# A seventh buffer for gate and up weights, in two parts, and three sets of gathered rows in a routed expert phase

## The chip, the cores and the metric

The kernel runs on one core of one Trainium2 chip. Its time is device microseconds (us) of one execution. Before the change it is 1276.21 us, the median of 3 runs (1276.14 to 1276.45). One execution was profiled: it took 1278.38 us, and its trace spans 1276.8 us. All positions below ("at 1066.34") are us from the start of that span.

## The reference, cut to what matters

One layer of an encoder for 1024 prompt frames and 32 sample frames: two kinds of attention side by side, and then a mixture of experts. Only the mixture and the routing ahead of it are touched by the order of the work. Everything is float32.

```python
def hier_moe(h, w_rg, b_rg, w_re, b_re, w_gate, w_up, w_down):
    g_sel = argmax(softmax(h @ w_rg + b_rg))            # 1 of 4 groups
    top_i = top_k(e_logits[g_sel], 2)                   # 2 of its 8 experts
    a = einsum('sd,edf->sef', h, w_gate)                # D_MODEL 1024, D_EXPERT 256, 32 experts
    b = einsum('sd,edf->sef', h, w_up)
    act = silu(a) * b * gates[:, :, None]
    return einsum('sef,efd->sd', act, w_down)
```

An expert's weights are w_gate and w_up (1 MiB each) and w_down (1 MiB): 96 MiB for the 32 experts.

## The kernel before, in words

The kernel is a row of phases. `phase_fr` (L1953) multiplies the attention's outputs with w_out, norms, and routes each frame to two experts; it writes the normed rows to `h2_dram` and the lists of (row, weight) per expert to `list_dram`. `phase_g` computes the experts. Between phases all engines meet.

`expert_blocks()` cuts the experts' lists into 23 blocks of 128 rows. Experts are named by a position p: 0 to 3 are known when the program is written, 17 and 31 (EARLY) are known early in routing, all others come from a table that routing sorts. The blocks, with the positions whose rows they hold: 0: 17+31; 1: 0; 2: 13+27; 3: 1; 4: 5+22; 5: 6+22; 6: 7+22; 7: 19+8; 8: 20+8; 9: 21+8; 10: 2; 11: 14+28; 12: 3; 13: 15+29; 14: 9+26; 15: 10+26; 16: 11+26; 17: 4; 18: 23+12; 19: 24+12; 20: 25+12; 21: 18; 22: 16+30.

For a block b GpSimd gathers 128 rows (`rows_in`, an indirect DMA, L2682) into one of ROWSETS = 4 sets of rows, PE turns them (`rows_turned`, g_X, L2689), PE multiplies them with gate and up weights (`first_products`, g_GU, L2697), ScalarE and VectorE form the hidden rows, PE turns these (g_H, L2704) and multiplies them with the down weights (`second_products`, g_Y, L2714), VectorE weights the result (L2940) and GpSimd adds it to `y` (`results_out`, L2676). PE's order is written out: in turn b it does first_products(b), second_products(b-1), rows_turned(b+2), hidden_turned(b); in the last turns second_products(21) comes ahead of first_products(22). GpSimd does rows_in(s) and then results_out(s - LAG), LAG being ROWSETS + 2.

Weights lie in six buffers, each with a part for gate and up (`w_gu`, 16 KB a partition) and a part for down (`w_down`, 8 KB a partition). An expert gets one buffer for both (`place`), the one whose present holder's last block comes first; `instead[p]` is that last block. SyncE (SP) issues all weight loads from one queue in program order: `gate_up_in(p)` waits until gu_mm has counted block instead[p] and issues two DMAs of 1 MiB (L2552, L2553), `down_in(p)` waits for dn_mm likewise and issues one (L2558). A down load is put off until its wait is two blocks older than that of the next gate and up load:

```python
            for p in order[len(known):]:
                while left and instead[left[0]] + 2 <= instead[p]:
                    down_in(left.pop(0))
                gate_up_in(p)
                left.append(p)
```

The four known experts and the gate and up weights of 17 and 31 are issued in phase_fr, the down weights of 17 and 31 (d17, d31) at the start of phase_g when the first gathered rows are in. After them SP's order is, with g for a gate and up pair (2 MiB) and d for a down load (1 MiB):

g13 g27 g5 d13 d27 g22 g6 d5 g7 d22 d6 g19 d7 g8 d19 g20 g21 d8 g14 d20 d21 g28 d14 g15 g29 d28 g9 d15 d29 g26 g10 d9 g11 d26 d10 g4 g23 d11 g12 d4 d23 g24 d12 g25 g18 d24 g16 d25 d18 g30 d16 d30.

"Position n" of a load in this order means the MiB issued from g13 on, itself included: g13 is at 2, g27 at 4, d5 at 13, d22 at 16, g8 at 22, d19 at 23, d8 at 28, d26 at 52, d12 at 65, d24 at 70, d25 at 73, d30 at 78.

Of the kernel before, what the change touches and what calls it, by code (L numbers as in the profile page):

```python
# [31 lines left out]
P = 128  # L32
D = 1024
KD = D // P
# [33 lines left out]
ROWW = _at  # L68
# [1884 lines left out]
def phase_fr(nc, io, g):  # L1953

    with ExitStack() as stack:
# [141 lines left out]
        @block.gpsimd  # L2097
        def _(pool):
            step = Steps(pool, pool_step)
            step(nc.gpsimd.iota(rown, pattern=[[1, LROWS]], base=0, channel_multiplier=LROWS))  # L2100
            step(nc.gpsimd.iota(i32[:], pattern=[[1, NE]], base=0, channel_multiplier=0))
            for k in range(2):
                step(nc.gpsimd.iota(pair[:, :, k, 0], pattern=[[P, NT]], base=0, channel_multiplier=1))
            for xg in g.xg:
                nc.gpsimd.memset(xg[:], 0.0)
            pool.wait_ge(oT_mm, 1)
            nc.gpsimd.memset(g.sample_region[:], 0.0)
            pool.wait_ge(z_out, 16)
# [484 lines left out]
def phase_g(nc, io, g):  # L2593

    with ExitStack() as stack:
        m = Memory(nc, stack)
        FT = DE // P
        ROWSETS = 4
        HALVES = (slice(0, D // 2), slice(D // 2, D))
        blocks = expert_blocks()  # L2600
        NB = len(blocks)
        wgu, wd = g.w_gu, g.w_down
        SLOTS = len(wgu)
# [8 lines left out]
        place, nth, instead = {}, {}, {}  # L2612
        holding = {}
        known = list(range(FIXED)) + list(EARLY)
        order = known + [p for p in order if p not in known]
        for q, p in enumerate(order):
            s = q if q < SLOTS else min(holding, key=lambda x: last_block[holding[x]])
            instead[p] = last_block[holding[s]] if q >= SLOTS else None
            nth[p] = sum(1 for x in place if place[x] == s)
            place[p], holding[s] = s, p  # L2620
        li = g.li + [m.sb(f"g_li{b}", [P, 2], U32) for b in range(3, NB)]
        l_li = m.sb("g_l_li", [P, 2], U32)
        xg = g.xg + [g.early[:, 0:D], g.sample_region]
        spare = 2 * KD * DE + 2 * D
        xT = g.first_region[:, spare:spare + 2 * KD * P].rearrange("p (b k t) -> p b k t", b=2, k=KD)
        sig = m.sb("g_sig", [P, DE])
# [12 lines left out]
        xT_mm, xT_done, gu_mm, sig_done, hid_done, hT_mm, hT_done, dn_mm, y_done, st_y, dve_step, started, l_side = m.sems(  # L2639
            "g_xT_mm g_xT_done g_gu_mm g_sig_done g_hid_done g_hT_mm g_hT_done g_dn_mm g_y_done g_st_y g_dve_step "  # L2640
            "g_started l_side")
# [50 lines left out]
        def gate_up(b, slots):  # L2692

            n = P // len(slots)
            for k in range(KD):
                for h, s in enumerate(slots):
                    end = nc.tensor.matmul(GU[h * n:h * n + n, :], lhsT=xT[:, b, k, h * n:h * n + n], rhs=wgu[s][:, :, k, :],  # L2697
                                           start=k == 0, stop=k == KD - 1, tile_position=(0, h * n))
            return end

# [18 lines left out]
        def lists(b):  # L2719
            return 16 * len(blocks[b])  # L2720

        def slots_of(b):

            unit = min(n for _, _, n, _ in blocks[b])
            return [place[p] for p, _, n, _ in blocks[b] for _ in range(n // unit)]

        @block.sync
        def _(sp):
            experts = {r: r * EPG for r in range(FIXED)}

            def expert(r):
                if r not in experts:
                    experts[r] = sp.value_load(g.order[0:1, r:r + 1], min_val=0, max_val=NE - 1)
                return experts[r]

            def gate_up_in(p):
                sp.wait_ge(gu_mm, instead[p] + 1)
                load_gate_up(nc, io, g, sp, expert(p), place[p], wgu_in[place[p]])

            def down_in(p):  # L2740
                sp.wait_ge(dn_mm, instead[p] + 1)
                load_down(nc, io, g, sp, expert(p), place[p], wd_in[place[p]])

            for b in (1, 2):
                load_list(g, sp, blocks[b], {p: expert(p) for p, *_ in blocks[b]}, li[b], li_in[b])
            sp.wait_ge(xg_in[0], 16)
            for p in EARLY:
                load_down(nc, io, g, sp, expert(p), place[p], wd_in[place[p]])
# [62 lines left out]
        def _(pe):  # L2811
            def first_products(b):
                for p, _, _, _ in blocks[b]:
                    pe.wait_ge(wgu_in[place[p]], 32 * nth[p] + 32)
                pe.wait_ge(xT_done, b + 1)
                if b:
                    pe.wait_ge(hid_done, b)
                gate_up(b % 2, slots_of(b)).then_inc(gu_mm, 1)

            def rows_turned(b):  # L2820
                pe.wait_ge(xg_in[b % ROWSETS], 16 * (b // ROWSETS) + 16)
# [3 lines left out]

            def second_products(b):
                for p, _, _, _ in blocks[b]:
                    pe.wait_ge(wd_in[place[p]], 16 * nth[p] + 16)
                pe.wait_ge(hT_done, b + 1)
                if b >= 2:  # L2830
                    pe.wait_ge(y_done, b - 1)
                if b == NB - 1:
                    down(b % 2, slots_of(b), lambda half: half.then_inc(dn_mm, 1)).then_inc(dn_mm, 1)
                else:
                    down(b % 2, slots_of(b)).then_inc(dn_mm, 1)

            def hidden_turned(b):
                pe.wait_ge(hid_done, b + 1)
# [168 lines left out]
def program(nc, io):  # L3007
    USED.clear()
    g = Shared()
    with ExitStack() as stack:  # L3010
# [14 lines left out]
        g.tri = m.sb("tri", [P, P])  # L3025
        g.ones = m.sb("ones", [P, P])
        g.eps = m.sb("eps", [P, 1])
        g.rows = m.sb("rows", [P, ROWW])
# [3 lines left out]
        g.ckv_new = m.sb("ckv_new", [P, KR])  # L3032
        g.vecT = m.sb("vecT", [P, 80])
        g.silu_c = m.sb("silu_c", [P, KD, 32])
# [62 lines left out]
        g.wgu_in = m.sems("wgu_in0 wgu_in1 wgu_in2 wgu_in3 wgu_in4 wgu_in5")  # L3097
        g.wd_in = m.sems("wd_in0 wd_in1 wd_in2 wd_in3 wd_in4 wd_in5")
        g.w_gu, g.w_down = [], []

# [11 lines left out]
        g.xg = [m.sb(f"g_xg{r}", [P, D]) for r in range(2)]  # L3112
        g.li = [m.sb(f"g_li{b}", [P, 2], U32) for b in range(3)]
        g.li_in = m.sems("g_li_in0 g_li_in1 g_li_in2")
        g.late = m.sb("late", [P, 12 * D])
        for part in (g.late[:, 0:6 * D], g.late[:, 6 * D:]):
            g.w_gu.append(part[:, 0:2 * KD * DE].rearrange("p (w k n) -> p w k n", w=2, k=KD))
            g.w_down.append(part[:, 2 * KD * DE:].rearrange("p (k n) -> p k n", n=D))
        phase_fr(nc, io, g)
        phase_g(nc, io, g)  # L3120
        mixed.close()
# [43 lines left out]
```

## Time and profile before

| what | value |
|---|---|
| median of 3 runs | 1276.21 us |
| the profiled execution | 1278.38 us |
| its span | 1276.8 us |
| PE busy over the span | 1165.3 us, 91% |
| VectorE, ScalarE, GpSimd busy | 714.7, 350.7, 214.6 us |
| expert phase, first gather to end | 967.8 to 1276.8 |

In the page, "PE" is the matrix engine, "SPq" SyncE's queue of instructions. An idle time ahead of an instruction is shown in square brackets with what ended it; "issue" means that the trace shows no releaser. A wait for a weight load often shows so, since the landing of such a load has no record of its own for each buffer. "DMA" in a table by stretches is the mean busy share of the core's 16 DMA engines.

### The profile page before, as it was taken

How to read it: one execution, taken by the hardware profiler on the slowest of the kernel's cores; microseconds unless marked ns; L12 is line 12 of the kernel's file. 1: busy time of each engine (PE TensorE's matmuls, PEld its weight loads, DVE VectorE, ACT ScalarE, POOL GpSimd, SP SyncE). 2: the span in 40 equal slices, each digit the busy share in tenths (PEclk: the TensorE clock that was granted, in tenths of full speed). 3: DMA queues.
4: the chain of work that ended last, by engine and by line, in shares of the span. 5: the costliest groups of instructions: out<-in, count | busy, mean ns of one | idle time of the engine just before them, and what ended most of it. 6: DMA issues, size and time to landing. Idle time of an engine off the chain costs nothing. (4 is left out here: it accounts for less than half of the span.)

```text
span 1276.8 us, 18764 instructions
## 1 busy us (share of the span) xinstructions
PE 1165.3 (91%) x7144; PEld 655.0 (51%) x7145; DVE 714.7 (56%) x1386; ACT 350.7 (27%) x770; POOL 214.6 (17%) x250
## 2 busy tenths in 40 slices
PE   4899999999968997799999999899976998999996
PEld 1456455564544556566677767555553332343332
DVE  1647476573756885467777686544472353544444
ACT  1113132141223444266555544223331000000000
POOL 0000000000400002254443333010122121222111
PEclk9899999999988998789999999899986999999998
DMA  8802223032257879421111005362565999999993
GB/s 362 328 17 88 71 61 114 17 88 59 67 158 237 300 276 274 124 60 30 30 30 31 1 1 168 97 246 84 192 250 179 398 382 369 363 388 391 351 327 79
DMA packets 103275, 226.17 MB, mean 177 GB/s; under 512 B 21034, under 2 KB 61212, under 8 KB 87826
## 3 DMA queue, kind: packets, MB, share of 16 engines
q1 hardware_dynamic: 92562, 207.61, 45.3%
q0 software_dynamic: 7344, 17.33, 5.5%
q8 instruction: 58, 0.95, 0.3%
q10 hardware_dynamic: 3280, 0.02, 0.1%
q14 instruction: 31, 0.25, 0.1%
HBM read 192.37 MB, written 39.38 MB: 182 GB/s over the span
## 5 line engine op out<-in xcount | busy, mean ns | idle before, releaser
L2142 PE MATMUL f_C<-first_region,oT 128*128 128x512 f32 x256 | 114.7, 601 | 0.0
L2922 DVE TENSOR_TENSOR g_sig<-g_GU,g_sig 128x256 f32<-128x256 f32 x23 | 9.8, 425 | 156.3 <-ACT g_sig L2873 156.3
L2697 PE MATMUL g_GU<-w_gu,first_region 128*32 128x512 f32 (+2 forms) x448 | 86.1, 604 | 6.0 <-issue 4.8
L2697 PE MATMUL g_GU<-late,first_region 128*32 128x512 f32 (+2 forms) x384 | 87.6, 606 | 4.3 <-issue 4.3
L1922 DVE TENSOR_TENSOR_SCAN region<-region,early 128x128 f32<-128x128 f32 (+7 forms) x64 | 88.5, 1403 | 5.0 <-POOL region L1726 4.9
L2142 PEld LDWEIGHTS f_C<-first_region,oT 128*128 128x128 f32 x256 | 47.8, 192 | 54.0 <-issue 53.8
L2676 POOL DMA_INDIRECT y<-oT,g_li x22 | 34.9, 1586 | 216.3 <-DVE oT L2940 208.7
L1791 PE MATMUL e_Z<-first_region,region 104*128 104x512 f32 (+3 forms) x192 | 70.5, 505 | 0.3 <-ACT region L1884 0.3
L1734 POOL TENSOR_SCALAR region<-region,e_sm 128x128 f32<-128x128 f32 (+7 forms) x64 | 47.0, 745 | 130.3 <-DVE e_sm L1935 130.3
L457 POOL MEMSET first_region<- 8x8448 f32 x1 | 7.1, 7132 | 316.0 <-PE U L495 316.0
L1928 DVE TENSOR_REDUCE e_sm<-e_Z 128x1 f32<-128x128 f32 (+7 forms) x64 | 46.5, 747 | 23.1 <-PE e_Z L1791 22.1
L2873 ACT ACTIVATE g_sig<-g_GU 128x256 f32<-128x256 f32 x23 | 8.8, 383 | 181.4 <-PE g_GU L2697 181.4
L1884 ACT ACTIVATE region<-e_Z,e_sm 128x128 f32<-128x128 f32 (+7 forms) x64 | 47.2, 749 | 11.3 <-DVE e_sm L1928 11.2
L2697 PEld LDWEIGHTS g_GU<-w_gu,first_region 128*32 128x32 f32 (+2 forms) x448 | 25.2, 119 | 48.0 <-issue 46.0
L1791 PEld LDWEIGHTS e_Z<-first_region,region 104*128 104x128 f32 x192 | 33.8, 198 | 29.8 <-issue 26.5
L495 PE MATMUL U<-first_region,values 128*128 128x512 f32 x96 | 44.9, 612 | 2.5 <-DVE values L893 2.5
L1862 ACT ACTIVATE region<-e_Z 128x128 f32<-128x128 f32 (+7 forms) x64 | 38.1, 649 | 33.0 <-PE e_Z L1770 33.0
L2714 PE MATMUL g_Y<-late,early 128*32 128x512 f32 (+2 forms) x192 | 45.3, 615 | 0.7 <-ACT early L2876 0.7
L2697 PEld LDWEIGHTS g_GU<-late,first_region 128*32 128x32 f32 (+2 forms) x384 | 25.8, 125 | 38.3 <-issue 37.9
L1770 PE MATMUL e_Z<-region 64*128 64x512 f32 (+3 forms) x192 | 41.1, 533 | 4.5 <-ACT region L1884 2.4
L1726 POOL TENSOR_SCALAR region<-region 128x128 f32<-128x128 f32 (+7 forms) x64 | 42.0, 672 | 14.2 <-ACT region L1862 13.2
L2113 POOL DMA_INDIRECT list_dram<-f_pair,f_dest x18 | 19.4, 1080 | 145.2 <-DVE f_dest L2505 142.5
(550 smaller groups left out, 2399.8 us busy)
## 6 DMA issues: line engine op xcount, KB each, us to landing
region<-w_ada SPq DMA_DIRECT2D x16, 1024.0 KB, 6.3
late<-w_gate SPq DMA_DIRECT2D x14, 1024.0 KB
late<-w_up SPq DMA_DIRECT2D x14, 1024.0 KB
late<-w_down SPq DMA_DIRECT2D x14, 1024.0 KB
w_gu<-w_gate SPq DMA_DIRECT2D x12, 1024.0 KB
w_gu<-w_up SPq DMA_DIRECT2D x12, 1024.0 KB
w_down<-w_down SPq DMA_DIRECT2D x12, 1024.0 KB, 21.5
region<-w_in SPq DMA_DIRECT2D x3, 2048.0 KB, 17.2
```

The lines of the kernel that those rows point to most:

```text
L495: end = nc.tensor.matmul(dst[:, :], lhsT=rows[:, k, :], rhs=weights(k), start=k == 0, stop=k == HALF - 1)
L1726: nc.gpsimd.tensor_scalar(part, part, -0.5, 0.5, ALU.mult, ALU.add).then_inc(left_done, 1)
L1734: nc.gpsimd.tensor_scalar(part, part, sm[:, n % 2, 4 + hh:5 + hh], 1.0, ALU.mult, ALU.mult).then_inc(scaled, 1)
L1770: end = nc.tensor.matmul(Z[:, hh, at + c:at + c1], lhsT=q_s[r, b, p, :], rhs=keys[r, p, c:c1], start=True, stop=True)
L1791: end = nc.tensor.matmul(Z[:, hh, at + c:at + c1], lhsT=g.q_hidden[:, b, h, :], rhs=g.kT_hidden[:, h, c:c1], start=True, stop=True)
L1862: nc.scalar.activation(stick[:, n % 2, hh, 0:W], Z[:, hh, at:at + W], ACT.Tanh, scale=0.5 * SB_SCALE).then_inc(tanh_done, 1)
L1884: nc.scalar.activation(w[:, hh, to:to + W], Z[:, hh, at:at + W], ACT.Exp, bias=sm[:, n % 2, hh:hh + 1], accum_out=sm[:, n % 2, 2 + hh:3 + ...
L1922: nc.vector.tensor_tensor_scan(back, back, least, 1.0, ALU.mult, ALU.max).then_inc(scan_done, 1)
L1928: nc.vector.tensor_reduce(sm[:, n % 2, hh:hh + 1], Z[:, hh, at:at + (t + 1) * P], AX.X, ALU.max, negate=True).then_inc(max_done, 1)
L2142: end = nc.tensor.matmul(C[n % 2][:, c * 512:(c + 1) * 512], lhsT=g.oT[:, i, k, :], rhs=wo[:, k, c * 512:(c + 1) * 512], start=k == 0, sto ...
L2697: end = nc.tensor.matmul(GU[h * n:h * n + n, :], lhsT=xT[:, b, k, h * n:h * n + n], rhs=wgu[s][:, :, k, :], start=k == 0, stop=k == KD - 1 ...
L2714: end = nc.tensor.matmul(Y[b][h * n:h * n + n, c * 512:(c + 1) * 512], lhsT=hT[:, b, k, h * n:h * n + n], rhs=wd[s][:, k, c * 512:(c + 1) ...
```

## The change

- There are seven places for gate and up weights and still six for down weights. The two kinds are planned apart (`plan(APART + 1)`, `plan(APART)`), so an expert's gate and up weights and its down weights can lie in different buffers.
- The seventh place is in two parts of 8 KB a partition each, `g.passing` and `g.apart`; four of the eight k slices of gate and up lie in each. Five experts land in it: 13, 7, 14, 11, 16. Their loads are four DMAs of 512 KB, with 4 KB a partition, instead of two of 1 MiB.
- `g.passing` also holds what earlier phases use (tri, ones, rows, ckv_new, vecT, silu_c), each of which was a tensor of its own. `g.apart` takes the room of two row sets.
- ROWSETS is 3: the sets are early, sample_region and a new tensor of phase_g. GpSimd clears the new one at the start of phase_g, ahead of its first gather; the clearing of two sets in phase_fr is gone. LAG becomes 5.

```diff
-            for xg in g.xg:
-                nc.gpsimd.memset(xg[:], 0.0)
...
-        ROWSETS = 4
+        ROWSETS = 3
...
-        for q, p in enumerate(order):
-            s = q if q < SLOTS else min(holding, key=lambda x: last_block[holding[x]])
-            instead[p] = last_block[holding[s]] if q >= SLOTS else None
+        def plan(buffers):
+            place, nth, instead, holding = {}, {}, {}, {}
+            for q, p in enumerate(order):
+                s = q if q < buffers else min(holding, key=lambda x: last_block[holding[x]])
+                instead[p] = last_block[holding[s]] if q >= buffers else None
+                nth[p] = sum(1 for x in place if place[x] == s)
+                place[p], holding[s] = s, p
+            return place, nth, instead
+
+        place_gu, nth_gu, instead_gu = plan(APART + 1)
+        place_d, nth_d, instead_d = plan(APART)
+
+        def weights_at(s, k):
+            return wgu[s][:, :, k, :] if s < APART else g.two_parts[k // (KD // 2)][:, :, k % (KD // 2), :]
+
+        def two_halves(name, e):
+            return io[name][e].rearrange("(p c k) n -> p c k n", p=P, c=2)
+
+        def gate_up_count(p):
+            return (32 if place_gu[p] < APART else 64) * (nth_gu[p] + 1)
...
-        xg = g.xg + [g.early[:, 0:D], g.sample_region]
+        xg = [g.early[:, 0:D], g.sample_region, m.sb("g_xg2", [P, D])]
...
             def gate_up_in(p):
-                sp.wait_ge(gu_mm, instead[p] + 1)
-                load_gate_up(nc, io, g, sp, expert(p), place[p], wgu_in[place[p]])
+                if instead_gu[p] is not None:
+                    sp.wait_ge(gu_mm, instead_gu[p] + 1)
+                if place_gu[p] < APART:
+                    load_gate_up(nc, io, g, sp, expert(p), place_gu[p], wgu_in[place_gu[p]])
+                    return
+                for w, name in enumerate(("w_gate", "w_up")):
+                    for c, part in enumerate(g.two_parts):
+                        sp.dma_start(part[:, w], two_halves(name, expert(p))[:, c]).then_inc(wgu_in[APART], 16)
...
-                while left and instead[left[0]] + 2 <= instead[p]:
+                while left and instead_gu[p] is not None and instead_d[left[0]] + 2 <= instead_gu[p]:
                     down_in(left.pop(0))
...
         def _(pool):
+            nc.gpsimd.memset(xg[2][:], 0.0).then_inc(cleared, 1)
+
             def rows_in(b):
+                if b == 2:
+                    pool.wait_ge(cleared, 1)
```

SP's order after d17 and d31 follows from the two plans:

g13 g27 g5 g22 d13 d27 g6 g7 d5 g19 d22 d6 g8 d7 g20 d19 g21 g14 d8 g28 d20 d21 g15 d14 g29 g9 d28 g26 d15 d29 g10 g11 d9 g4 d26 d10 g23 g12 d11 g24 d4 d23 g25 d12 g18 g16 d24 g30 d25 d18 d16 d30.

In it g13 has no wait on a block; g27 and g5 wait for block 0, g22 for block 1, d13 and d27 for block 0's second products; g21 and g14 wait for block 6.

## Rows read from the trace of the kernel before

**Rows 1.** The page: busy time of PE over the span.
```profile
PE 1165.3 (91%) x7144; PEld 655.0 (51%) x7145; DVE 714.7 (56%) x1386; ACT 350.7 (27%) x770; POOL 214.6 (17%) x250
```

**Rows 2.** Busy time by stretches: start:end length, engines, PEclk, DMA share, GB/s.
```profile
986.00:1230.00 244.00, 230.73 (x1540) 91.86 (x1544) 106.80 (x155) 15.31 (x40) 49.01 (x38) 0.99 1.01 375
974.00:990.00 16.00, 14.28 (x57) 6.56 (x57) 4.43 (x5) 0.77 (x2) 4.95 (x5) 0.80 0.68 232
780.00:785.00 5.00, 5.00 (x64) 4.26 (x59) 3.33 (x6) 1.89 (x6) 2.22 (x2) 1.00 1.05 398
```

**Rows 3.** Timeline of PE in the expert phase, instructions with idle time ahead.
```profile
1002.59 0.65 PE L2697 MATMUL g_GU<-late,first_region 128*64 128x512 f32 x2 [2.96 <-issue]
...
1066.34 1.07 PE L2697 MATMUL g_GU<-w_gu,first_region 128*32 128x512 f32 x3 [4.84 <-issue]
...
1152.56 0.63 PE L2697 MATMUL g_GU<-oT,first_region 128*32 128x512 f32 x3 [2.40 <-issue]
...
1171.88 0.63 PE L2714 MATMUL g_Y<-oT,early 128*32 128x512 f32 x3 [0.34 <-issue]
...
1201.68 0.63 PE L2697 MATMUL g_GU<-late,first_region 128*32 128x512 f32 x3 [1.29 <-issue]
...
1214.62 0.63 PE L2697 MATMUL g_GU<-w_gu,first_region 128*32 128x512 f32 x3 [1.12 <-DMA w_gu<-w_up]
```

**Rows 4.** DMA queues, 986 to 1230: packets, MB, share of 16 engines.
```profile
q1 hardware_dynamic: 10606, 77.30, 78.0%
q0 software_dynamic: 5328, 14.04, 22.0%
```

**Rows 5.** Single down loads on SP's queue: time of issue, then us to landing.
```profile
L2558 SPq DMA_DIRECT2D w_down<-w_down x1: 333/333/333, 1013.3 to 1013.3; - x1
DMA to landing us min/median/max: 19.3/19.3/19.3
...
L2558 SPq DMA_DIRECT2D w_down<-w_down x1: 333/333/333, 1048.5 to 1048.5; - x1
DMA to landing us min/median/max: 21.5/21.5/21.5
...
L2558 SPq DMA_DIRECT2D w_down<-w_down x1: 2245/2245/2245, 1137.1 to 1137.1; - x1
DMA to landing us min/median/max: 34.7/34.7/34.7
...
L2558 SPq DMA_DIRECT2D oT<-w_down x1: 3671/3671/3671, 1182.8 to 1182.8; - x1
DMA to landing us min/median/max: 34.3/34.3/34.3
...
L2558 SPq DMA_DIRECT2D w_down<-w_down x1: 2053/2053/2053, 1211.1 to 1211.1; - x1
DMA to landing us min/median/max: 31.0/31.0/31.0
```

**Rows 6.** GpSimd: the clearing of two row sets; the first gather of phase_g.
```profile
L2105 POOL MEMSET g_xg<- x2: 957/958/959, 792.0 to 792.9; 128x1024 f32 x2
...
967.78 1.04 POOL L2682 DMA_INDIRECT g_xg<-h_dram,g_li  x1 [8.21 <-DMA g_li<-list_dram]
```

**Rows 7.** Chain of waits: start, us, what.
```profile
1044.98 3.43 PE g_Y L2714 x32
...
1066.34 8.42 PE g_GU L2697 x64
...
1086.53 3.43 PE g_Y L2714 x32
...
1091.29 7.00 PE g_GU L2697 x64
...
1233.46 3.43 PE g_Y L2714 x32
```

**Rows 8.** Clock: stretch with the longest wait; columns as in rows 2.
```profile
1060.00:1070.00 10.00, 5.16 (x38) 2.40 (x38) 2.88 (x3) 0.38 (x1) 2.62 (x2) 0.83 1.03 390
```

**Rows 9.** DMA issues 850 to 1277: KB each, us to landing.
```profile
h_dram<-late SPq DMA_DIRECT2D x6, 512.0 KB, 2.7
```

More of the change, by code:

```diff
@@ L2602, in phase_g @@
         wgu, wd = g.w_gu, g.w_down
-        SLOTS = len(wgu)
+        APART = len(wgu)
         order = []
@@ L2611, in phase_g @@
                 last_block[p] = b
-        place, nth, instead = {}, {}, {}
-        holding = {}
         known = list(range(FIXED)) + list(EARLY)
         order = known + [p for p in order if p not in known]
-        for q, p in enumerate(order):
-            s = q if q < SLOTS else min(holding, key=lambda x: last_block[holding[x]])
-            instead[p] = last_block[holding[s]] if q >= SLOTS else None
-            nth[p] = sum(1 for x in place if place[x] == s)
-            place[p], holding[s] = s, p
+        def plan(buffers):
[14 more added lines that the diff above has]
+            return (32 if place_gu[p] < APART else 64) * (nth_gu[p] + 1)
         li = g.li + [m.sb(f"g_li{b}", [P, 2], U32) for b in range(3, NB)]
         l_li = m.sb("g_l_li", [P, 2], U32)
-        xg = g.xg + [g.early[:, 0:D], g.sample_region]
+        xg = [g.early[:, 0:D], g.sample_region, m.sb("g_xg2", [P, D])]
         spare = 2 * KD * DE + 2 * D
@@ L2638, in phase_g @@
         Y = [m.ps(f"g_Y{b}", [P, D]) for b in range(2)]
-        xT_mm, xT_done, gu_mm, sig_done, hid_done, hT_mm, hT_done, dn_mm, y_done, st_y, dve_step, started, l_side = m.sems(
+        xT_mm, xT_done, gu_mm, sig_done, hid_done, hT_mm, hT_done, dn_mm, y_done, st_y, dve_step, started, l_side, cleared = m.sems(
             "g_xT_mm g_xT_done g_gu_mm g_sig_done g_hid_done g_hT_mm g_hT_done g_dn_mm g_y_done g_st_y g_dve_step "
-            "g_started l_side")
+            "g_started l_side g_cleared")
         wgu_in, wd_in = g.wgu_in, g.wd_in
@@ L2696, in gate_up @@
                 for h, s in enumerate(slots):
-                    end = nc.tensor.matmul(GU[h * n:h * n + n, :], lhsT=xT[:, b, k, h * n:h * n + n], rhs=wgu[s][:, :, k, :],
+                    end = nc.tensor.matmul(GU[h * n:h * n + n, :], lhsT=xT[:, b, k, h * n:h * n + n], rhs=weights_at(s, k),
                                            start=k == 0, stop=k == KD - 1, tile_position=(0, h * n))
@@ L2720, in lists, with slots_of @@
             return 16 * len(blocks[b])
-        def slots_of(b):
+        def slots_of(b, place):
             unit = min(n for _, _, n, _ in blocks[b])
@@ L2736, in gate_up_in @@
             def gate_up_in(p):
-                sp.wait_ge(gu_mm, instead[p] + 1)
-                load_gate_up(nc, io, g, sp, expert(p), place[p], wgu_in[place[p]])
+                if instead_gu[p] is not None:
[6 more added lines that the diff above has]
+                        sp.dma_start(part[:, w], two_halves(name, expert(p))[:, c]).then_inc(wgu_in[APART], 16)
             def down_in(p):
-                sp.wait_ge(dn_mm, instead[p] + 1)
-                load_down(nc, io, g, sp, expert(p), place[p], wd_in[place[p]])
+                sp.wait_ge(dn_mm, instead_d[p] + 1)
+                load_down(nc, io, g, sp, expert(p), place_d[p], wd_in[place_d[p]])
             for b in (1, 2):
@@ L2747, in _ @@
             for p in EARLY:
-                load_down(nc, io, g, sp, expert(p), place[p], wd_in[place[p]])
+                load_down(nc, io, g, sp, expert(p), place_d[p], wd_in[place_d[p]])
             left = []
             for p in order[len(known):]:
-                while left and instead[left[0]] + 2 <= instead[p]:
+                while left and instead_gu[p] is not None and instead_d[left[0]] + 2 <= instead_gu[p]:
                     down_in(left.pop(0))
@@ L2813, in first_products @@
                 for p, _, _, _ in blocks[b]:
-                    pe.wait_ge(wgu_in[place[p]], 32 * nth[p] + 32)
+                    pe.wait_ge(wgu_in[place_gu[p]], gate_up_count(p))
                 pe.wait_ge(xT_done, b + 1)
@@ L2817, in first_products @@
                     pe.wait_ge(hid_done, b)
-                gate_up(b % 2, slots_of(b)).then_inc(gu_mm, 1)
+                gate_up(b % 2, slots_of(b, place_gu)).then_inc(gu_mm, 1)
             def rows_turned(b):
@@ L2827, in second_products @@
                 for p, _, _, _ in blocks[b]:
-                    pe.wait_ge(wd_in[place[p]], 16 * nth[p] + 16)
+                    pe.wait_ge(wd_in[place_d[p]], 16 * nth_d[p] + 16)
                 pe.wait_ge(hT_done, b + 1)
@@ L2832, in second_products @@
                 if b == NB - 1:
-                    down(b % 2, slots_of(b), lambda half: half.then_inc(dn_mm, 1)).then_inc(dn_mm, 1)
+                    down(b % 2, slots_of(b, place_d), lambda half: half.then_inc(dn_mm, 1)).then_inc(dn_mm, 1)
                 else:
-                    down(b % 2, slots_of(b)).then_inc(dn_mm, 1)
+                    down(b % 2, slots_of(b, place_d)).then_inc(dn_mm, 1)
             def hidden_turned(b):
@@ L3024, in program @@
         g.ident = m.sb("ident", [P, P])
-        g.tri = m.sb("tri", [P, P])
-        g.ones = m.sb("ones", [P, P])
+        g.passing = m.sb("passing", [P, 2 * D])
+        g.tri = g.passing[:, D:D + P]
+        g.ones = g.passing[:, D + P:D + 2 * P]
         g.eps = m.sb("eps", [P, 1])
-        g.rows = m.sb("rows", [P, ROWW])
+        g.rows = g.passing[:, 0:ROWW]
         g.modT = m.sb("modT", [P, 48, 2])
@@ L3031, in program @@
         g.scale_m = m.sb("scale_m", [P, KD, 2])
-        g.ckv_new = m.sb("ckv_new", [P, KR])
-        g.vecT = m.sb("vecT", [P, 80])
-        g.silu_c = m.sb("silu_c", [P, KD, 32])
+        g.ckv_new = g.passing[:, D + 2 * P:D + 2 * P + KR]
+        g.silu_c = g.passing[:, D + 4 * P:D + 6 * P].rearrange("p (k b) -> p k b", b=32)
+        g.vecT = g.passing[:, D + 6 * P:D + 6 * P + 80]
         g.w_in_loaded = m.sems("w_lat_loaded w_v_loaded w_q_loaded w_k_loaded")
@@ L3096, in program @@
         g.longest = m.sb("longest", [1, 1], I32)
-        g.wgu_in = m.sems("wgu_in0 wgu_in1 wgu_in2 wgu_in3 wgu_in4 wgu_in5")
+        g.wgu_in = m.sems("wgu_in0 wgu_in1 wgu_in2 wgu_in3 wgu_in4 wgu_in5 wgu_in6")
         g.wd_in = m.sems("wd_in0 wd_in1 wd_in2 wd_in3 wd_in4 wd_in5")
@@ L3111, in program @@
         g.y = turned[:, 6 * KD * P:8 * KD * P].rearrange("p (b n) -> p b n", b=2)
-        g.xg = [m.sb(f"g_xg{r}", [P, D]) for r in range(2)]
+        g.apart = m.sb("apart", [P, 2 * D])
         g.li = [m.sb(f"g_li{b}", [P, 2], U32) for b in range(3)]
@@ L3118, in program @@
             g.w_down.append(part[:, 2 * KD * DE:].rearrange("p (k n) -> p k n", n=D))
+        g.two_parts = [part[:].rearrange("p (w k n) -> p w k n", w=2, k=KD // 2) for part in (g.passing, g.apart)]
         phase_fr(nc, io, g)
```

## The prediction

> **What bounds the kernel now.** I read the page first, then the stretches, then PE's timeline, then the loads. PE is busy 91% of the span [rows 1], and in the expert phase, 986 to 1230, it is busy 230.7 of 244 us while the 16 DMA engines are at 1.01, that is full [rows 2]. Both are near their limit, so the question is which one waits for the other. PE's timeline answers: it has six idle times there, five ahead of first products and one ahead of second products, of 2.96, 4.84, 2.40, 0.34, 1.29 and 1.12 us, 12.95 us in all [rows 3]. Behind the longest the clock has fallen (0.83 in that stretch, between its levels of 2.4 and 1.2 GHz) [rows 8], and the first products take 8.42 us instead of 7.00, another 1.42 [rows 7]. So 14.37 us of this phase are PE waiting for weights.
>
> That they are waits for loads in their order is seen by counting positions. The six waits end at position 4 (g27), 22 (g8), 46 (g26), 52 (d26), 60 (g12) and 64 (g24). From 1002.59 to 1066.34 that is 63.75 us for 18 MiB, 3.54 us each; from 1066.34 to 1214.62 148.3 us for 42, 3.53 each [rows 3]. Single down loads lie on the same line: d5 (13) lands at 1013.3 + 19.3 = 1032.6, d19 (23) at 1070.0, d26 (52) at 1171.8, d12 (65) at 1217.1, d25 (73) at 1242.1 [rows 5]. SP's loads are one stream, delivered in order of issue at a steady pace from 986 to about 1230. A buffer more can't make the stream faster. It can start it earlier, and it changes who stands ahead of whom in it.
>
> **Part 1: the earlier start.** g13 no longer waits for block 0; it follows d17 and d31. From 974 to 990 the DMA engines are at 0.68, so 16 x 0.32 = 5.1 us of them are idle [rows 2]. The loads' own pace is 77.30 MB in 0.78 x 244 = 190 us, 406 GB/s [rows 2, 4], so g13 (2.10 MB) needs 5.2 us and just fits. Against it stands part 2. I take 4.0 us of lead for the whole stream; between 0 (nothing of the gap used) and 5.1.
>
> **Part 2: the clearing.** It now stands ahead of GpSimd's first gather, at the point where all engines wait for it. It takes 0.96 us, and the gather starts at 967.78 with PE idle behind it [rows 6]. I take the whole 0.96 us, for the first rows, for d17, d31 and g13; it could be 0 if it fits under the wait for the list, and is hardly over 1.1. That part of the lead is taken off in the 4.0. The clearing removed from phase_fr lay beside PE's work: 0.
>
> **Part 3: the order.** Compare the two orders: every down load from d13 to d18 now has two MiB more ahead of it. d22 goes from position 16 to 18, d8 from 28 to 30, d26 from 52 to 54, d24 from 70 to 72. Gate and up loads stand up to 2 MiB earlier (g8 22 to 21, g26 46 to 44, g12 60 to 59, g24 64 to 62). Two MiB are 5.2 us at 406 GB/s, the lead is 4.0: the down loads land 1.2 us later than before. So the gate and up loads are out of the way, and the question becomes how much room the down loads had.
>
> **Part 4: half pieces.** Five experts load in pieces of 512 KB with 4 KB a partition. w_out, loaded with 2 KB a partition, moved at 398 GB/s [rows 2], against 406. For 10 MiB that is 26.3 against 25.8 us: between 0 and 0.5, I take 0.3 by d24, 0.15 by d8, behind a filled queue. The far end is a piece that overlaps nothing: 2.7 us from issue to landing [rows 9] against 1.3 us of moving, 1.4 us for each of 20 pieces, 28 us; with several MiB outstanding all the time I give that nothing. SP's ten additional issues lie beside a full queue: 0.
>
> **Part 5: three row sets.** Gather b is issued behind result b-6 instead of b-7, and is needed in turn b-2, three turns (35 us) later: not late. One gather fewer stands beside the stream at a given moment. Queue 0 takes 22% of 244 us for 38 gathers and result transfers [rows 2, 4], 1.4 us each. So between 0 and -1.4 for a down load in the middle; I take -0.7, and 0 for d24, by when all gathers are done either way.
>
> **The sum, turn by turn.** Offsets are to the profiled execution.
> - Block 2: before, ready at 1002.59 - 2.96 = 999.63, waited for g27. Now ready at 1000.6; g27 lands 4 us earlier, 998.6. No wait. Offset -2.0.
> - Second products of block 4 started at 1044.98 [rows 7], now ready at 1043.0. They need d22: before, at 1032.6 + 3 x 3.74 = 1043.8 (3.74 us each between d5 and d19). Now 1.2 + 0.1 - 0.7 = 0.6 later, 1044.4. Wait 1.4, offset -0.6.
> - First products of block 7: the 4.84 and the 1.42 are gone (g8, at 21, about 1058.6). Second products of block 7 are ready at 1086.53 - 4.84 - 1.42 - 0.6 = 1079.7. They need d8. Six MiB behind g8, at (1171.8 - 1070.0) / 29 = 3.51 each, it is due at 1087.4; PE did not wait at 1086.53 [rows 7], so it landed just before. I take 1086.5, and now 0.7 later, 1087.2. Wait 7.5 us. A wait longer than 4.84 brings the clock down again: +1.4. Offset +2.1.
> - Block 14: the 2.40 is gone (g26 at 44), offset -0.3. Its second products, ready at 1171.54 - 0.3 = 1171.2, need d26: 1171.8 + 0.7 = 1172.5. Offset +0.6.
> - Blocks 18 and 19: 1.29 and 1.12 gone. Offset -1.8.
> - Second products of block 19 started at 1233.46 [rows 7], now ready at 1231.7. They need d24. Before, between d12 (65) and d25 (73), 3.13 us each: 1232.7. Now 1.2 + 0.3 later, 1234.2. Wait 2.5. Offset +0.7.
> - d25 (1242.1 before) and later ones have their room, and the tail is unchanged.
>
> The span becomes 1276.8 + 0.7 = 1277.5 and the profiled time 1279.1. The medians lie 2.2 us below that execution, so 1276.21 + 0.7 = 1276.9 us. The 14.4 us of waits for gate and up weights turn into about 12 us of waits for down weights, the clearing and the clock.
>
> Bounds: d24 before at the earliest 1230.1 (1217.1 + 5 x 2.6, nothing beside the stream) and at the latest 1233.46; its delay between 0 and 5.7. d26's delay is at least -1.4, which leaves the start of block 14's second products at 1170.4, offset -1.5, and -3.9 after the two waits that go. So -3.9 to +5.8.
>
> **The rivals.**
> - *Full gain.* The down loads are in time and all waits go: -14.4 + 1.0 = -13.4, 1262.8 us. For it: only 0.34 us of the waits seen are for a down load. Against: the row of 1171.88 is itself a down load that PE waited for, and by the count d8 and d24 landed within a microsecond of their use. It needs d8 by 1079.7, 7 us before its place in the stream. Chance 0.07.
> - *Part of it.* Down loads delayed by nothing and d24 early: -1.8 to -3.9, 1272.3 to 1274.4. It decides at a landing of d24 before 1231. Chance 0.18, half of it beyond -2.55.
> - *The lead is not won.* g13's load collides in 974 to 986 with d17, d31, four gathers and the lists, and only moves them; down loads are then 5.2 + 0.3 later, d24 lands at 1238.2, offset +4.7, 1280.9 us. It decides where g13 lands after about 988, and is slower than the measurement can miss once d24 lands after 1236.0. For it: a gather waits for its list in that stretch [rows 6]. Chance 0.22.
> - *The half pieces are slow.* In this trace no 512 KB load stands in a full queue. At twice the cost of the w_out row (1.0 us) the end moves by +1.4. Chance 0.05.
>
> On the half pieces the Trainium skill speaks against the change: "DMA: Bandwidth & Descriptors", section Bandwidth, asks for 1 MiB or more per DMA and gives 341 GB/s for a 1 MB one. No run here shows 512 KB loads alone, and the trace disagrees for 1 MiB ones in a full queue (406 GB/s). By the page's figure, an estimate, 10 MiB would take 30.8 us instead of 25.8, and the end would be at about +5.4, 1281.6 us.
>
> **How the numbers follow.** A measurement of this kernel tells 0.2%, 2.55 us, from no change. The forecast, down loads take over as the wait and the end moves by -1.8 to +3, has 0.48. Faster by over 0.2% needs the full gain or the far half of the part gain: 0.07 + 0.09 = 0.16. Slower by over 0.2%: the lead not won 0.22, a slow-piece share 0.02 and 0.06 of the forecast's upper end, 0.30. Within: 0.54. The range goes from 1273.0 to 1281.5: it leaves out the full gain, and little on either side.
>
> **What would show it.** Right: no idle ahead of first products of blocks 2, 7, 14, 18, 19; 5 us or more ahead of the second products of block 7 (g_Y, near 1080 to 1087), smaller ones at blocks 4, 14 and 19, with the clock down once; DMA share near 1 already from 976. The first gather about 1 us later. Wrong: no idle ahead of g_Y near 1080 (full gain), or DMA still idle at 982 to 986 (lead not won), or first products that still wait.

## The result, and the profile after

The changed kernel takes 1281.61 us in the median of 7 runs (1280.54 to 1286.65), against 1276.76 for the kernel before in the same runs (1276.14 to 1278.49). The ratio is 1.0043, 95% interval 1.003 to 1.0056: slower by some 5 us, outside the stated range by 0.1 us. The profiled execution took 1285.22 us, 3.6 above the median, its span is 1283.6. The ratios here and below leave out the executions in the slow state (1298 us and more); the medians in the table below hold all.

The page after, busy time of PE, and PE's four idle times of the expert phase, from the timeline (they answer to [rows 1, 3]):

```profile
PE 1169.3 (91%) x7144; PEld 655.0 (51%) x7145; DVE 713.3 (56%) x1386; ACT 350.5 (27%) x770; POOL 213.8 (17%) x249
```

```profile
1049.20 1.07 PE L2727 MATMUL g_Y<-w_down,early 128*32 128x512 f32 x3 [5.45 <-issue]
...
1090.36 0.63 PE L2727 MATMUL g_Y<-w_down,early 128*32 128x512 f32 x3 [3.13 <-issue]
...
1175.07 0.63 PE L2727 MATMUL g_Y<-oT,early 128*32 128x512 f32 x3 [1.96 <-issue]
...
1237.95 0.63 PE L2727 MATMUL g_Y<-w_down,early 128*32 128x512 f32 x3 [3.87 <-DMA w_down<-w_down]
```

Not one idle time is left ahead of first products (g_GU); five of the six before were there. All four are ahead of second products (g_Y), at blocks 4, 7, 14 and 19, the blocks the prediction named. They sum to 14.41 us, against 12.95 before. The time PE waits has moved from one kind of weights to the other. It has hardly grown: in two more traces of the changed kernel (e1 and e12) it is 14.53 and 12.20 us. What has grown is the time lost to the clock behind the waits, below.

The stretches (columns as in [rows 2]) show that the earlier start was won: from 974 to 990 the DMA engines are at 0.94 instead of 0.68. The gap itself lay from 982 to 986; the first row is the kernel before, the others are the change.

```profile
982.00:986.00 4.00, 4.00 (x21) 1.17 (x18) 0.00 (x0) 0.02 (x1) 0.70 (x1) 1.00 0.26 82
```

```profile
982.00:986.00 4.00, 4.00 (x20) 1.36 (x18) 0.00 (x0) 0.00 (x0) 0.00 (x0) 0.92 0.99 336
974.00:990.00 16.00, 14.27 (x59) 6.79 (x58) 4.22 (x5) 0.71 (x2) 3.32 (x4) 0.73 0.94 329
986.00:1230.00 244.00, 233.15 (x1542) 90.87 (x1540) 106.80 (x155) 15.33 (x40) 49.77 (x38) 0.99 1.00 371
1050.00:1060.00 10.00, 10.00 (x74) 3.56 (x70) 2.42 (x2) 0.38 (x1) 1.70 (x2) 0.78 0.88 354
```

The last row is the stretch behind the first wait: the granted clock is 0.78, between the levels of 1.2 and 2.4 GHz. The chain of waits has the price: the second products of blocks 4 and 19 take 6.17 and 5.34 us, where they took 3.43 before [rows 7].

```profile
1043.75 5.45 issue
1049.20 6.17 PE g_Y L2727 x32
```

```profile
1237.95 5.34 PE g_Y L2727 x32
```

Start of the expert phase: SP's first list load of the phase, GpSimd's clearing, and the first gather 0.16 us behind it. PE turns the first rows at 973.42, against 972.13 before.

```profile
968.08 2.97 SPq L2562 DMA_DIRECT2D g_li<-list_dram  x3
```

```profile
968.06 0.95 POOL L2791 MEMSET g_xg<- 128x1024 f32 x1 [6.38 <-POOLq L1955]
969.17 1.05 POOL L2695 DMA_INDIRECT early<-h_dram,g_li  x1 [0.16 <-issue]
...
973.42 0.91 PE L2702 MATMUL g_X<-ident,early 128*128 128x128 f32 x3 [8.33 <-DMA early<-h_dram,g_li]
```

Executions of one and the same kernel turn their first rows at quite different times (968 to 976 over the traces below), so below "the expert phase" is the time from that moment to the end of the span: 304.7 us before (1276.8 - 972.1), 310.2 after (1283.6 - 973.4).

### The profile page after: what moved, and what is told of

Read it like the earlier page. It is cut to its first block and busy times, and to the rows that moved or that the text cites. A ratio compares the mean times of both kernels' runs of the same rounds, so it can differ in the third digit from the quotient of the medians.

```text
span 1283.6 us, 18791 instructions
## 1 busy us (share of the span) xinstructions
PE 1169.3 (91%) x7144; PEld 655.0 (51%) x7145; DVE 713.3 (56%) x1386; ACT 350.5 (27%) x770; POOL 213.8 (17%) x249
## 5 line engine op out<-in xcount | busy, mean ns | idle before, releaser
L2710 PE MATMUL g_GU<-late,first_region 128*32 128x512 f32 (+1 forms) x400 | 86.8, 605 | 0.0
L2727 PE MATMUL g_Y<-w_down,early 128*32 128x512 f32 (+2 forms) x224 | 47.9, 657 | 12.4 <-issue 8.6
L2963 DVE SCALAR_TENSOR_TENSOR oT<-g_Y,g_li,g_share 128x1024 f32<-128x1024 f32 (+1 forms) x24 | 29.8, 1240 | 23.7 <-PE g_Y L2727 23.0
```

What stands on the lines that cost most here:

```text
L2727: end = nc.tensor.matmul(Y[b][h * n:h * n + n, c * 512:(c + 1) * 512], lhsT=hT[:, b, k, h * n:h * n + n], rhs=wd[s][:, k, c * 512:(c + 1) ...
```

## The experiments

All medians are of runs beside the kernel before on the same chip; ratios are to it. Positions are in MiB, counted as ahead of the prediction. One execution of each run was traced, and it is not always a typical one: those of the change and of e1 lie 3.6 and 4.7 us above their medians, those of e2, e5, e3 and e6 3.7, 5.1, 3.2 and 2.8 below.

| run | kernel | median | ratio, interval | traced: first rows, expert phase |
|---|---|---|---|---|
| e1 | the change again | 1282.18 | 1.0051, 1.0036 to 1.0065 | 975.9, 309.4 |
| e12 | the change a third time | 1284.22 | 1.006, 1.0039 to 1.0082 | 974.2, 306.3 |
| e2 | change, old order | 1276.61 | 1.0002, 0.9989 to 1.0016 | 970.9, 300.4 |
| e5 | change, rule + 1 | 1275.03 | 0.999, 0.9975 to 1.0006 | 969.1, 299.4 |
| e10 | e5 again | 1276.33 | 0.9993, 0.9977 to 1.0009 | 975.1, 299.7 |
| e7 | change, rule + 3 | 1303.82 | 1.0213, 1.0183 to 1.0243 | 970.5, 329.6 |
| e6 | change, g13 late | 1286.21 | 1.007, 1.0044 to 1.0096 | 973.1, 308.8 |
| e9 | e5, clearing later | 1276.09 | 0.9999, 0.9984 to 1.0014 | 974.0, 301.1 |
| e13 | e9, stream earlier | 1275.2 | 0.9998, 0.9983 to 1.0013 | 972.3, 301.3 |
| e3 | before, five in halves | 1277.6 | 1.0, 0.9987 to 1.0013 | 968.3, 304.5 |
| e11 | before, all in halves | 1285.12 | 1.006, 1.0038 to 1.0083 | 973.5, 310.0 |
| e4 | before, shared tensor | 1277.72 | 1.0006, 0.9994 to 1.0018 | 973.1, 303.4 |
| e8 | before, three sets | 1277.8 | 1.0013, 0.9999 to 1.0026 | 971.3, 304.5 |
| e14 | before, e4 and e8 | 1277.64 | 1.0009, 0.9994 to 1.0024 | 968.9, 304.8 |

**e2, the order undone.** Only the rule by which SP puts off down loads is the old one; seventh buffer, halves, clearing and row sets stay.

```diff
-                while left and instead_gu[p] is not None and instead_d[left[0]] + 2 <= instead_gu[p]:
+                while left and instead_d[left[0]] + 2 <= instead_d[p]:
```

> The changed kernel with SP's loads in the order of the kernel before (seventh buffer, half pieces, clearing and three row sets stay). Theory order: the lead of g13 now counts for all loads; d22, d8, d26, d24 are back at positions 16, 28, 52, 70 and land 3 us or more earlier than before. The waits of second products of blocks 4, 7 and 14 are 1 us or less, and the kernel is faster than before the change: 1272 to 1275 us. Theory half pieces, or clearing and early phases: the order doesn't matter, it stays at 1280 us or above.

Against the change the median falls by 5 to 6 us, to that of the kernel before, and the traced expert phase by 9.8 us. So the order makes the slowdown: with everything else of the change in place and the old order, it is gone. The kernel is not faster than before in the median, as the expectation had said it would be; only its phase is shorter (300.4 against 304.7). PE's idle times in the timeline of e2: the long waits ahead of g_Y at blocks 4 and 19 are gone, 1.32 and 2.34 us remain at blocks 7 and 14, and g_GU waits again for 1.92, 1.11, 0.31 and 2.75 us.

```profile
1059.45 0.63 PE L2710 MATMUL g_GU<-w_gu,first_region 128*32 128x512 f32 x3 [1.92 <-issue]
...
1079.62 0.63 PE L2727 MATMUL g_Y<-w_down,early 128*32 128x512 f32 x3 [1.32 <-issue]
...
1165.90 0.63 PE L2727 MATMUL g_Y<-oT,early 128*32 128x512 f32 x3 [2.34 <-issue]
...
1209.29 1.06 PE L2710 MATMUL g_GU<-late,first_region 128*32 128x512 f32 x8 [2.75 <-DMA late<-w_up]
```

One down load shows both terms. d9 lands, counted from the first rows turned, at 191.1 us before (1126.6 + 36.6 - 972.1), at 184.3 in e2 and at 190.8 in the change. These are its rows on SP's queue, time of issue and us to landing, before, in e2 (first rows turned at 970.94) and in the change (973.42):

```profile
L2558 SPq DMA_DIRECT2D oT<-w_down x1: 2060/2060/2060, 1126.6 to 1126.6; - x1
DMA to landing us min/median/max: 36.6/36.6/36.6
```

```profile
L2556 SPq DMA_DIRECT2D oT<-w_down x1: 2383/2383/2383, 1119.1 to 1119.1; - x1
DMA to landing us min/median/max: 36.1/36.1/36.1
```

```profile
L2556 SPq DMA_DIRECT2D oT<-w_down x1: 589/589/589, 1132.8 to 1132.8; - x1
DMA to landing us min/median/max: 31.4/31.4/31.4
```

By position, e2 against the kernel before is the lead (6.8 us at d9, 5.4 at d11, 4.2 at d12, 3.7 at d18), and the change against e2 is two positions (6.5, 6.3, 6.4 and 5.9 us at the same four). Each figure is a difference of two traces. Those with the old order and the old start (before, e3, e4, e8, e14) differ among themselves by 1.4 us at d9 and 1.9 at d11. And e6, below, divides the same delay in another way.

**e5 and e10, the rule one block shorter.** The rule of the change with + 1.

```diff
-                while left and instead_gu[p] is not None and instead_d[left[0]] + 2 <= instead_gu[p]:
+                while left and instead_gu[p] is not None and instead_d[left[0]] + 1 <= instead_gu[p]:
```

> The changed kernel with the rule for putting off a down load one block shorter (+ 1 instead of + 2): d22, d8, d26, d24 at positions 16, 26, 52, 68. Theory order: as with the old order, waits of second products small, first gathered rows turned to end of span 300 to 302 us (before 304.7, change 310.2, old order 300.4), 5 us or more faster than the change. Theory early phases or clearing: 1280 us or above.

> e5 once more, beside e9 on the same chip. Its first trace had an expert phase of 299.4 us, 5.3 less than before, but its median was only 0.3 us below the kernel before. Theory order: the expert phase is again 299 to 301 us, and what is missing in the median is in the phases ahead of it. Rival: that trace was a lucky one, and this one shows 303 us or more.

The traced expert phase is 299.4 and 299.7 us, so it was no lucky trace. The medians are 0.3 us below the kernel before, in both, with intervals that hold 1, and in one comparison e10 lies 7.9 us below the change (e12). In e5's timeline the longest waits are 2.50 and 2.28 us:

```profile
1057.17 0.63 PE L2710 MATMUL g_GU<-w_gu,first_region 128*32 128x512 f32 x3 [2.50 <-issue]
...
1163.26 0.83 PE L2727 MATMUL g_Y<-oT,early 128*32 128x512 f32 x3 [2.28 <-issue]
```

Short as they are, the clock is down behind both, at 0.66 and 0.68 (PEclk in the stretches below), and the products behind the first take 8.77 us instead of 7.00:

```profile
1057.00:1062.00 5.00, 4.83 (x32) 1.71 (x36) 0.00 (x0) 0.00 (x0) 1.40 (x2) 0.66 1.03 386
1163.20:1168.50 5.30, 5.24 (x32) 1.59 (x32) 1.47 (x2) 0.00 (x0) 0.00 (x0) 0.68 1.01 409
```

```profile
1057.17 8.77 PE g_GU L2710 x64
```

**e7, the rule one block longer.** As e5's edit, with + 3 in place of + 2.

> The changed kernel with the rule one block longer (+ 3): most down loads have another 2 MiB ahead of them (d8 at 32, d26 at 56, d24 at 74), which doubles the suspected cost. Theory order: 6 us more for the down loads and more waits ahead of second products, 1287 to 1293 us. Theory half pieces, clearing or layout: no change against the changed kernel.

The direction is as expected and the size is at least double: 22 us over e1 in the median. PE's idle times ahead of g_Y are 12.63, 0.98, 10.24 and 10.21 us. One reason is in the order itself. The expectation has d26 at 56; by the rule it is at 58, and nine of the 24 down loads that the rule moves at + 2 have four MiB more ahead than in the change, not two, among them d27 and d26, which the first and the last of the three long waits are for. That the rest is slack used up at + 2 is argued, not shown.

```profile
1029.72 1.12 PE L2727 MATMUL g_Y<-late,early 128*64 128x512 f32 x2 [12.63 <-issue]
...
1102.40 1.07 PE L2727 MATMUL g_Y<-w_down,early 128*32 128x512 f32 x3 [10.24 <-issue]
...
1197.08 1.07 PE L2727 MATMUL g_Y<-oT,early 128*32 128x512 f32 x3 [10.21 <-issue]
```

**e6, the lead given up.** The new order, but g13 waits for block 0.

```diff
-                if instead_gu[p] is not None:
-                    sp.wait_ge(gu_mm, instead_gu[p] + 1)
+                sp.wait_ge(gu_mm, (instead_gu[p] or 0) + 1)
```

> The changed kernel, but g13 waits for block 0 as it did before the change, so that the lead is given up and the new order stays. Theory order with lead: the stream loses what the old order won against the kernel before, 4 to 7 us, so the expert phase takes 314 to 317 us and the time is 1285 to 1290 us. Theory that the lead was never won: no change against the changed kernel, 310 us and 1281 to 1285 us.

The median is within what was expected, 4.0 us above e1's and 2.0 above e12's, neither in one comparison with it. But the intervals of the ratios overlap (1.0044 to 1.0096, and 1.003 to 1.0082 over the three runs of the change), and the traced phase (308.8 us) lies among those of the change (306.3 to 310.2), where the rival had it. So the time doesn't show what the lead is worth in the new order. The DMA engines are at 0.66 from 974 to 990, as before the change:

```profile
974.00:990.00 16.00, 14.27 (x59) 6.74 (x58) 4.43 (x5) 0.77 (x2) 3.77 (x4) 0.75 0.66 221
```

d12 shows the lead, first in e6 (first rows turned at 973.13), then in the change: it lands at 249.9 and at 247.2 us, counted from the first rows turned.

```profile
L2556 SPq DMA_DIRECT2D oT<-w_down x1: 2979/2979/2979, 1185.3 to 1185.3; - x1
DMA to landing us min/median/max: 37.7/37.7/37.7
```

```profile
L2556 SPq DMA_DIRECT2D oT<-w_down x1: 1797/1797/1797, 1181.7 to 1181.7; - x1
DMA to landing us min/median/max: 38.9/38.9/38.9
```

That is a lead of 2.7 us at d12, and at d9 it is 0.8, less than e2 gives. Two positions without a lead are e6 against the old order and start: 0.5 us at d9, 4.9 at d12, and 6.5 at d24 (the end of PE's wait for it in e6, 1239.52, against its landing in e14).

"The lead is not won" is the rival whose 1280.9 us, and 1238.2 for d24, lie nearest to the result (1281.61, and 1237.9). That is luck: its condition, DMA engines idle from 982 to 986, is not met in the change (0.99, against 0.26 before).

**e3 and e11, half pieces.** The kernel before; five experts, then all 26, in pieces of 512 KB.

```diff
+        HALVED = (13, 7, 14, 11, 16)          # e11: tuple(order[len(known):])
...
+                for w, name in enumerate(("w_gate", "w_up")):
+                    src = io[name][expert(p)].rearrange("(p c k) n -> p c k n", p=P, c=2)
+                    for c in range(2):
+                        sp.dma_start(g.w_gu[place[p]][:, w, c * (KD // 2):(c + 1) * (KD // 2)], src[:, c]).then_inc(
+                            wgu_in[place[p]], 16)
```

> The kernel before, with gate and up weights of the five experts 13, 7, 14, 11 and 16 loaded in four DMAs of 512 KB (4 KB a partition) instead of two of 1 MiB; nothing else. Theory half pieces: 2 to 5 us slower, 1278.5 to 1281.5 us, with g8 landing 1 us or more after 1066.3. Theory order: 0 to +0.6, 1276.8 us.

> The kernel before with gate and up weights of all 26 later experts in 512 KB pieces: five times the half pieces of the change. Theory half pieces: 2 us or more slower. Theory order: 0 to 2.5 us (0.5 us for each 10 MiB at the pace of w_out), 1276 to 1278 us.

Five in halves can't be told from none. All in halves cost 0.6%, more than the 0 to 2.5 us of the order theory. The stream's pace shows why: 73.28 MB in 0.771 x 244 = 188.1 us, 390 GB/s, against 406 before [rows 4] and 404 in the change (76.12 MB in 0.772 x 244). The rows are e11's and the change's queue 1, from 986 to 1230:

```profile
q1 hardware_dynamic: 17002, 73.28, 77.1%
```

```profile
q1 hardware_dynamic: 11742, 76.12, 77.2%
```

The 390 is a mean: a third of e11's bytes, the down loads, still comes in 1 MiB pieces. At 390 instead of 406 GB/s the 81.8 MB of the whole stream take some 8 us more; the phase grew by 5.3 (310.0 against 304.7), and where the rest met slack isn't followed up. For the change's five, 404 instead of 406 over the same 81.8 MB is 1.0 us; e3's stream, the same five in the old order, is at 404 too (76.73 MB in 0.779 x 244).

**e4, e8 and e14, the other parts.** The kernel before with the shared tensor (e4), with ROWSETS = 3 and `xg = g.xg + [g.early[:, 0:D]]` (e8), with both (e14).

> The kernel before, with tri, ones, rows, ckv_new, vecT and silu_c inside one tensor as in the change; nothing else. Theory early phases (where these tensors lie costs time in the phases that use them): the first gather of the expert phase starts 1 to 2 us later and the time is 1 to 2 us longer. Theory order: no change, 1276.2 to 1277.0 us; what the first trace of the change had there is scatter between executions.

> The kernel before with three row sets (LAG 5), nothing else. Theory order: 0 within the measurement, expert phase 304 to 305.5 us. Theory row sets (gathers come too late or at a bad time): PE waits ahead of g_X, slower by 2 us or more.

> The kernel before with the shared tensor and three row sets together. Apart they gave ratios of 1.0006 and 1.0013, each with an interval that touches 1. If the 4 us that are missing between the expert phase of the repaired orders (4 to 5 us shorter) and their medians (0.3 us) lie here: ratio 1.002 or more, 1279 us. If not: within 0.1% of the kernel before.

None moves by more than its interval, and the expert phase is that of the kernel before in all three (303.4, 304.5, 304.8). All three medians lie 0.8 to 2.5 us above the kernel before; a cost of 1 us together isn't excluded.

e14's trace also holds landings that the trace before lacks. Counted from its first rows turned (968.91), d22 lands at 69.6 us and d24 at 259.9; in the change (973.42) at 75.7 and 264.5. The rows are d22 and d24 in e14, then the same in the change:

```profile
L2558 SPq DMA_DIRECT2D late<-w_down x1: 333/333/333, 1019.8 to 1019.8; - x1
DMA to landing us min/median/max: 18.7/18.7/18.7
...
L2558 SPq DMA_DIRECT2D w_down<-w_down x1: 2310/2310/2310, 1195.2 to 1195.2; - x1
DMA to landing us min/median/max: 33.6/33.6/33.6
```

```profile
L2556 SPq DMA_DIRECT2D late<-w_down x1: 333/333/333, 1023.7 to 1023.7; - x1
DMA to landing us min/median/max: 25.4/25.4/25.4
...
L2556 SPq DMA_DIRECT2D w_down<-w_down x1: 4250/4250/4250, 1207.1 to 1207.1; - x1
DMA to landing us min/median/max: 30.8/30.8/30.8
```

**e9, the clearing later.** e5 with the clearing behind the first two gathers.

```diff
-            nc.gpsimd.memset(xg[2][:], 0.0).then_inc(cleared, 1)
-
             def rows_in(b):
                 if b == 2:
+                    nc.gpsimd.memset(xg[2][:], 0.0).then_inc(cleared, 1)
                     pool.wait_ge(cleared, 1)
```

> The order of e5 (+ 1), and the clearing of the third row set moved behind GpSimd's first two gathers. Theory clearing on the path: the gap between the last list transfer and the first gather is 0.8 to 1.0 us shorter than in e5 and so is the time: 1274.0 us against e5's 1275.0, 1 to 2 us below the kernel before. Theory that it hides under the wait for the list: no change against e5.

No difference to e10 beside it (1276.09 and 1276.33). The traces are sharper than the times. From the last list transfer of routing to the first gather the scatter covers all: 8.49 us in e9 (961.28 to 969.77), and with the clearing ahead 7.99 to 9.11 in the change, e1, e10 and e12. Counted from SP's first list load of phase_g instead, which is issued as the phase begins, the gather starts 1.08 or 1.09 us later in all eight traces with the clearing ahead (968.08 to 969.17 in the change), and 0.89 to 0.97 in the eight without (966.87 to 967.78 before, 968.87 to 969.77 in e9). So most of the clearing's 0.95 us fits under the wait for the list, and it costs 0.2 us. The row of the kernel before:

```profile
966.87 2.97 SPq L2564 DMA_DIRECT2D g_li<-list_dram  x3
```

**e13, the stream earlier.** e9 without SP's wait for the first gathered rows ahead of d17 and d31.

> The order of e5, the clearing behind the first two gathers, and d17, d31 and g13 issued without waiting for the first gathered rows, so that the stream starts some 3 us earlier. Theory order and lead: every load lands up to 3 us earlier against the first rows turned, the expert phase takes 297 to 299 us and the time is 1272 to 1274 us, below both kernels. Rival: the stream collides with the first gathers and lists, the first rows are turned 2 us or more later, and nothing is won.

Nothing is won, as its rival said, but not in the rival's way. The first rows are turned at 972.32, no later than elsewhere. It is the second gather that lands late: PE is idle 3.64 us ahead of the second rows, where it is 1.41 in all others, and the phase takes 301.3 us instead of 299.4 to 301.1:

```profile
977.93 0.91 PE L2702 MATMUL g_X<-ident,o_s 128*128 128x128 f32 x3 [3.64 <-DMA o_s<-h_dram,g_li]
```

**e1 and e12, the change again.**

> The changed kernel once more. Its seven times lay in two groups, 1280.5 to 1281.6 and 1285.2 to 1286.7 us, with the profiled one in the upper. Theory order (two MiB more ahead of every down load): waits ahead of second products of blocks 4, 7, 14 and 19 in either group; the groups differ by whether these waits are long enough for the clock to fall behind them (2.7 and 1.9 us behind the waits of 5.45 and 3.87 us in the first trace), so 1280.6 or 1285.4 us. Theory early phases: the groups differ ahead of the expert phase, by the 1.3 to 2.1 us by which the first trace of the change was late at 973.

> The changed kernel a third time, for a trace from its lower group (1280.5 to 1282 us). Theory order: expert phase 306 to 308 us with waits ahead of the same four second products, and shorter ones than the 5.45 and 3.87 us of the first trace, so that the clock falls less. If the groups are made ahead of the expert phase: 310 us again, and the first rows are turned 3 to 4 us earlier than 973 to 976.

PE waits ahead of the second products of the same blocks (e1 without block 14), but the sizes wander from the first trace to e1 and e12: ahead of block 4's second products 5.45, 4.54 and 6.85 us, ahead of block 7's 3.13, 5.88 and 1.17. The phases are 310.2, 309.4 and 306.3 us. The two groups of times are no groups in e12 (1279.99 to 1289.86, spread evenly), and the first rows come at 974.2, neither early nor late. So the expected split explains nothing; what makes executions of this kernel differ by up to 10 us stays open.

## Why the prediction was wrong

The mechanism was as forecast, and a size was not. Point by point:

- *What bounds it: the order of one stream at a steady pace.* Right. Rules of + 1, + 2 and + 3 give 299.4 and 299.7, 306.3 to 310.2, and 329.6 us for the phase with everything else the same.
- *Waits ahead of first products go, second products of blocks 4, 7, 14 and 19 take over.* Right, all of them (the rows of the timeline).
- *The lead is 4.0 us.* Won, as the DMA engines show (0.99 from 982 to 986). Its size isn't settled: 6.8 us at d9 and 3.7 by d18 in the old order (e2 against before), 0.8 at d9 and 2.7 at d12 in the new one (the change against e6).
- *Two MiB are 5.2 us at 406 GB/s, less 4.0 of lead: down loads land 1.2 us later (1.5 for d24, 0.6 for d22).* This step failed, in the prediction's parts 3 and 5: the net delay of the down loads that PE waits for is too small. Forecast are landings of d22, d8, d26 and d24 at 1044.4, 1087.2, 1172.5 and 1234.2; the waits for them ended at 1049.20, 1090.36, 1175.07 and 1237.95, that is 4.8, 3.2, 2.6 and 3.8 us later. Nor is the delay one number for all: against e14, counted from the first rows turned, d7 lands 0.4 us later, d9 1.0, d24 4.6, d8 5.7, d22 6.1 and d5 6.6, all with two MiB more ahead.

  The likelier part is the price of a position. Two positions measure 5.9 to 6.5 us (e2 against the change) where 5.2 was taken, the loads' own pace. Gathers and result transfers go on meanwhile: with the 78% of the engines that queue 1 had before [rows 4], 5.2 us become 6.7, an estimate. The prediction had such a pace in its first part, 3.5 us a MiB as PE is served, and then used the other. No run takes the gathers out, and e6 puts two positions at 0.5, 4.9 and 6.5 us with a smaller lead, so how much of the error is the price and how much the lead stays open. The prediction also took off 0.7 us for one gather fewer, which no trace shows.
- *The clock falls once, behind block 7, for 1.4 us.* It fell behind block 4 (5.45 us of waiting, 2.7 lost) and behind block 19 (3.87 us, 1.9 lost), and not behind block 7 (3.13 us instead of the forecast 7.5, since block 4 had already made PE later; 0.2 lost). The loss behind block 19 counts in full, as nothing behind it had slack; that behind an earlier block shortens the waits that follow. The prediction let the clock fall only behind a wait longer than 4.84 us and so put the clock behind its own wait of 2.5 us at block 19 at nothing. That was no safe reason: waits of 2.50 and 2.28 us in e5 cost 1.8 and 1.9.
- *The clearing costs 0.96 us.* It costs 0.2, by the start of the gather in sixteen traces (under e9).
- *Half pieces cost 0.3 us.* More: 1.0 us by the pace of the change's own stream; in the median e3 can't tell. The prediction set 398 GB/s for w_out, bytes over time, beside 406, bytes over the engines' share; by the same measure w_out moved at 398 / 1.05 = 379 [rows 2], which would have made its upper bound of 0.5 some 1.8. The Trainium skill ("DMA: Bandwidth & Descriptors", section Bandwidth) gives its 341 GB/s for a single load of 1 MB issued from GpSimd. In a full queue issued from SP, e11 shows 390 GB/s with two thirds of the bytes in 512 KB loads: the direction of the rule on size holds, 4% slower, and the figure for one load doesn't carry over. The 1281.6 us that the prediction worked out from it are the measured median by luck, since five experts in halves alone (e3) cost nothing that can be measured.

The sum for the profiled execution: forecast offset +0.7; d24's lateness beyond it 1237.95 - 1234.2 = 3.75; the clock behind it 1.9; 0.4 in the tail. That is +6.8, the measured 1283.6 - 1276.8. In the medians the change is +4.85, and +0.7 was forecast.

What is not settled: the repaired orders have an expert phase 3.4 to 5.3 us shorter than before (301.3 to 299.4 against 304.7) and medians that are at most 1.5 us lower, with ratios of 0.999 to 1.0002. In the traces with the seventh buffer the first rows are turned at 972.9 in the mean of ten, in those without at 971.2 in the mean of six, with a scatter of 2 us in each. That may be the missing part; of it the clearing is 0.2, and the parts tried alone (e4, e8, e14, e9) don't show the rest.

## What to carry to other kernels

When a loading stream is the bound, another buffer for one kind of data doesn't speed it up; it only moves that data ahead of the other kind, so look for the load that is just in time now and count what newly stands in front of it. Price a place in the queue by the pace of delivery, everything that shares the engines included. And when buffers of two kinds are planned apart, the rule that interleaves their loads has to be written anew: here one digit of it was worth 5 to 8 us one way and some 20 the other.

## What the runs showed of the hardware

What an idle time costs TensorE behind it can't be read from its length alone. In the change waits of 3.13, 3.87 and 5.45 us cost 0.2, 1.9 and 2.7 us behind them (3.43 us of second products took 3.64, 5.34 and 6.17), and in the kernel before 4.84 us cost 1.42. But among the waits for weights of 2.01 to 3.21 us in all sixteen traces twelve cost at most 0.2 us and ten 1.7 to 1.9. The shortest that did, 2.01 us in e8, was followed by second products of 5.34 us at a granted clock of 0.67, between the two levels. What makes the difference no run shows.

A stream with two thirds of its bytes in loads of 512 KB (4 KB a partition) moved at 390 GB/s in a full queue; with all in loads of 1 MiB (8 KB a partition) it moved at 406.
